# Gate and up projections: the sum W21 + W22 made by the transfers instead of VectorE

## What is computed

```
h2 = rmsnorm(x, norm2_g)                                   # 512 x 1024
x  = x + (silu(h2 @ w_ffn_gate) * (h2 @ w_ffn_up)) @ w_ffn_down   # D_FF = 2816
return rmsnorm(x, final_g)
```

## Time and profile before

| | us |
|---|---|
| median of 3 runs | 698.44 (698.36 to 698.49) |
| the profiled execution | 698.02 |
| its span in the profile | 695.9 |
| busy in the span: PE, DVE, ACT, POOL | 674.3, 484.2, 378.6, 36.6 |
| mean granted clock of PE | 0.994 |

### The profile page before, as it was taken

How to read it: one execution, slowest core, us unless ns; L and a number is a source line. 1 busy time by engine, 2 the same in 40 slices (tenths; PEclk the granted TensorE clock), 3 DMA queues, 4 the chain that set the end, 5 groups by cost and what they waited for, 6 DMA issues and landing times.

```text
span 695.9 us, 10920 instructions
## 1 busy us (share of the span) xinstructions
PE 674.3 (97%) x4042; PEld 602.9 (87%) x4042; DVE 484.2 (70%) x781; ACT 378.6 (54%) x638; POOL 36.6 (5%) x42
## 2 busy tenths in 40 slices
PE   4999999999999999999997999999999999999996
PEld 4998888888888878888897999999999998888884
DVE  4686558787888885845698987878898763333346
ACT  6538577987787872223764545544555552322234
POOL 0000401111121200000000000000000000000000
PEclk9999999999999999999999999999999999999998
DMA  8242221122222226331272334444323313313103
GB/s 292 69 120 79 70 62 27 55 70 66 70 66 85 97 65 268 121 121 61 62 182 70 86 89 122 121 121 121 91 74 80 116 60 122 118 64 121 60 0 122
DMA packets 73694, 67.25 MB, mean 97 GB/s; under 512 B 5887, under 2 KB 64446, under 8 KB 73662
## 3 DMA queue, kind: packets, MB, share of 16 engines
q1 hardware_dynamic: 73646, 66.82, 31.6%
q10 hardware_dynamic: 16, 0.00, 0.0%
HBM read 64.72 MB, written 2.10 MB: 96 GB/s over the span
## 4 chain that ended last, share of the span: by engine, by line
PE 94%; DVE 3%; ACT 2%; DMA 1%; issue 0%; SPq 0%; ACTq 0%; DVEq 0%
PE ps L407 20%; PE ps L409 20%; PE ps L408 20%; PE ps L1704 9%; PE ps L1706 9%; PE ps L1707 9%; PE ps L1613 2%; PE ps L1445 1%; PE ps L1563 1%; PE ps L1560 1%; DMA xt<-in_x_dram 1%; DVE hT_lo L973 1%; DVE w_lo L1240 0%; ACT w_hi L302 0%; DVE f_lo L1251 0%
## 5 line engine op out<-in xcount | busy, mean ns | idle before, releaser
L407 PE MATMUL ps<-hT_hi,w_lo 128*128 128x512 f32 (+1 forms) x288 | 100.2, 348 | 1.1 <-DVE w_lo L312 0.6
L409 PE MATMUL ps<-hT_hi,w_hi 128*128 128x512 f32 (+1 forms) x288 | 98.6, 342 | 0.0
L408 PE MATMUL ps<-hT_lo,w_hi 128*128 128x512 f32 (+1 forms) x288 | 98.5, 342 | 0.0
L1704 PE MATMUL ps<-f_hi,w_lo 128*128 128x256 f32 x320 | 91.4, 286 | 3.9 <-DVE f_lo L1251 3.9
L1706 PE MATMUL ps<-f_lo,w_hi 128*128 128x256 f32 x320 | 91.2, 285 | 0.0
L1707 PE MATMUL ps<-f_hi,w_hi 128*128 128x256 f32 x320 | 91.1, 285 | 0.0
L312 DVE TENSOR_TENSOR w_lo<-raw,w_hi 128x1024 fp32r<-128x1024 f32 (+3 forms) x55 | 64.2, 1173 | 33.0 <-ACT w_hi L302 31.9
L302 ACT ACTIVATE w_hi<-raw 128x1024 fp32r<-128x1024 f32 (+3 forms) x55 | 53.6, 984 | 37.8 <-PE ps L409 36.5
L819 ACT ACTIVATE w_hi<-scr 128x1024 fp32r<-128x1024 f32 x50 | 51.9, 1057 | 37.2 <-PE ps L1707 36.0
L1235 DVE TENSOR_TENSOR w_lo<-raw,w_hi 128x1024 fp32r<-128x1024 f32 x22 | 26.9, 1225 | 63.4 <-ACT w_hi L806 63.4
L407 PE MATMUL ps<-w_hi,f_lo 128*128 128x512 f32 x180 | 70.0, 389 | 0.0
(11 more groups left out here) (195 smaller groups left out, 1501.4 us busy)
## 6 DMA issues: line engine op xcount, KB each, us to landing
raw<-in_w_in_dram SPq DMA_DIRECT2D x12, 1024.0 KB
raw<-in_w_ffn_down_dram SPq DMA_DIRECT2D x11, 1024.0 KB, 4.9
raw<-in_w_ffn_gate_dram SPq DMA_DIRECT2D x10, 512.0 KB, 4.7
raw<-in_w_ffn_up_dram SPq DMA_DIRECT2D x10, 512.0 KB, 5.3
scr<-in_w_ffn_gate_dram SPq DMA_DIRECT2D x10, 512.0 KB, 5.2
scr<-in_w_ffn_up_dram SPq DMA_DIRECT2D x10, 512.0 KB, 6.0
raw<-in_w_out_dram SPq DMA_DIRECT2D x4, 1024.0 KB
xt<-in_x_dram SPq DMA_DIRECT2D x4, 512.0 KB, 6.0
```

The lines of the kernel that those rows point to most:

```text
L407: nc.tensor.matmul(dst, l_lo, r_hi, start=start, stop=False)
L408: nc.tensor.matmul(dst, l_hi, r_lo, start=False, stop=False)
L409: return nc.tensor.matmul(dst, l_hi, r_hi, start=False, stop=stop)
L1704: nc.tensor.matmul(dst, wl[:, k, :], x_hi[:, k, :], start=start and k == 0, stop=False, skip_group_check=True)
```

## The change

S1 is no longer added by DVE. GpSimd issues, for each step and for gate and up each, a transfer of W21 (128 partitions of 4 rows of 512 bytes, 256 KB) to S1's place in `w_sum`, waits until it has landed (`st_base`), and issues a second transfer of W22 that adds to what stands there (`accum_op`), which counts `st_s1`. The first transfer for the next step waits until the low half of c (gate) or d (up) of this step is made, since S1's place is read until then. The sums of the first step are loaded much earlier, when attention no longer needs the place. The raw blocks are loaded as before, so W21 and W22 of every step come twice. The scratch space for GpSimd's transfer descriptors grows from 1024 to 4096 bytes.

On DVE `sums` falls apart: `third` (S3) stays where it was, `second` (S2 = S1 - W11) goes behind the two `corner`, and waits for `st_s1`. ACT's waits count the new order.

```diff
+            def first_sums(j, par, count, first=False):
+                col = slice(j * 256 + P * (2 + STEPS + par), j * 256 + P * (3 + STEPS + par))
+                for m, src in enumerate((w_fg_v, w_fu_v)):
+                    if not first:
+                        pool.wait_ge(w_ready, st_count("cd"[m], j, par - 1))
+                    nc.gpsimd.dma_start(s1_view(m), src[:, 0:4, col]).then_inc(st_base[m], 16)
+                for m, src in enumerate((w_fg_v, w_fu_v)):
+                    pool.wait_ge(st_base[m], count)
+                    nc.gpsimd.dma_start(s1_view(m), src[:, 4:8, col], accum_op=ALU.add).then_inc(st_s1[m], 16)
+
+            pool.wait_ge(vs_ready, HEADS)
+            first_sums(0, 0, 16, first=True)
+            first_sums(0, 1, 32)
+            for j in range(1, STEPS // 2):
+                for par in range(2):
+                    first_sums(j, par, j * 32 + 16 * par + 16)
...
-                nc.vector.tensor_tensor(out(c), w21, w22, ALU.add).then_inc(st_sum, 1)
-                nc.vector.tensor_tensor(out(4 + m), w11, w21, ALU.subtract).then_inc(st_sum, 1)
-                dve.wait_ge(st_sum, j * 16 + 8 * par + 3 * m + 1)
-                nc.vector.tensor_tensor(out(c + 1), out(c), w11, ALU.subtract).then_inc(st_sum, 1)
...
+            def second(m, j, par):
+                dve.wait_ge(st_s1[m], j * 32 + 16 * par + 16)
+                dve.wait_ge(st_in[par][m], j * 32 + 32)
+                nc.vector.tensor_tensor(w_sum[:, 2 * m + 1, :].rearrange("p (k n) -> p k n", k=4), s1_view(m),
+                                        st_raw(par, m)[:, 0:4, 0, :], ALU.subtract).then_inc(st_sum, 1)
...
                 block_lo("g", j, par)
                 corner(0, j, par)
                 if first:
-                    sums(1, nj, npar)
+                    third(1, nj, npar)
+                if not last:
+                    second(0, nj, npar)
                 corner(1, j, par)
+                if not last:
+                    second(1, nj, npar)
...
-    nc = _bacc.Bacc("TRN2", target_bir_lowering=False, num_devices=1, dynamic_dma_scratch_size=1024)
+    nc = _bacc.Bacc("TRN2", target_bir_lowering=False, num_devices=1, dynamic_dma_scratch_size=4096)
```

More of the change, by code:

```diff
@@ L330, in st_raw, with s1_view @@
             return flat.rearrange("p (k i n) -> p k i n", k=KD, i=2)
+        def s1_view(m):
+            return w_sum[:, 2 * m, :].rearrange("p (k n) -> p k n", k=4)
         def st_source(par, tile):
@@ L817, in block_hi @@
                 else:
-                    act.wait_ge(st_sum, j * 16 + 8 * par + {"c": 3, "d": 6, "e": 5, "f": 7, "g": 8}[tile])
+                    act.wait_ge(st_sum, j * 12 + 6 * par + {"e": 2, "c": 3, "d": 4, "f": 5, "g": 6}[tile])
                 nc.scalar.activation(st_split(w_hi, tile), st_source(par, tile), ACT.Copy).then_inc(w_half, 1)
@@ L1252, in t_lo, with third @@
                                         ALU.subtract).then_inc(t_split, 1)
[L1254 to L1260, removed]
-                dve.wait_ge(st_in[par][m], j * 32 + 32)
-                nc.vector.tensor_tensor(out(c), w21, w22, ALU.add).then_inc(st_sum, 1)
-                nc.vector.tensor_tensor(out(4 + m), w11, w21, ALU.subtract).then_inc(st_sum, 1)
-                dve.wait_ge(st_sum, j * 16 + 8 * par + 3 * m + 1)
-                nc.vector.tensor_tensor(out(c + 1), out(c), w11, ALU.subtract).then_inc(st_sum, 1)
+            def third(m, j, par):
+                v = st_raw(par, m)
+                dve.wait_ge(st_in[par][m], j * 32 + 32)
+                nc.vector.tensor_tensor(w_sum[:, 4 + m, :].rearrange("p (k n) -> p k n", k=4), v[:, 0:4, 0, :],
+                                        v[:, 0:4, 1, :], ALU.subtract).then_inc(st_sum, 1)
+            def second(m, j, par):
[3 more added lines that the diff above has]
+                                        st_raw(par, m)[:, 0:4, 0, :], ALU.subtract).then_inc(st_sum, 1)
             def fourth(m, j, par):
                 w12 = st_raw(par, m)[:, 4:8, 0, :]
-                dve.wait_ge(st_sum, j * 16 + 8 * par + 3 * m + 3)
+                dve.wait_ge(st_sum, j * 12 + 6 * par + 3 + m)
                 dve.wait_ge(w_ready, st_count("ab"[m], j, par))
@@ L1297, in step @@
                 feature = j * 2 + par + 2
+                if first:
+                    third(1, 0, 0)
+                    second(0, 0, 0)
+                    second(1, 0, 0)
                 block_lo("c", j, par)
-                if first:
-                    sums(1, 0, 0)
                 block_lo("d", j, par)
@@ L1310, in step @@
                     dve.wait_ge(w_ready, st_count("e", j, par))
-                    sums(0, nj, npar)
+                    third(0, nj, npar)
                 block_lo("f", j, par)
@@ L1361, in _ @@
             block_lo("b", 0, 0)
-            sums(0, 0, 0)
+            third(0, 0, 0)
             first_product(0)
```

1 line of the change is left out of this document (added).

## The result

The changed kernel takes 714.76 us (median of 4 runs, 712.59 to 716.86) against 698.47 for the kernel before beside it: ratio 1.0225, 95% interval 1.0203 to 1.0247. The forecast of no change was wrong. What came is the first rival, "the chain is too long", almost at the price of its example, 715 at L = 14. The profiled execution took 714.0 us, its span 712.1, which is 16.2 more than before.

The account below looks back on a forecast made before the run. PE was taken to bound the ordinary steps, with no hole. DVE's relief, the first step and the transfer chain summed as 0 + 0 + 0 on a median of 698.44: forecast 698.4 us, range 697.2 to 717.

Parts of the forecast that it names:

- the first rival: Ordinary steps: chain too long, DVE stands at `second` of up, PE waits; 715 at L = 14, 761 at most; chance 0.28.
- L: Time from the end of gate's low half of c to the landing of up's S1; taken 9.2 us, bounds 5.7 to 19.1.
- What bounds the kernel: Gate and up stage: PE busy for all 20.17 us of an ordinary step, so less DVE work gives nothing there.
- What leaves DVE: Twenty additions S1 of 0.686 us, 13.7 us busy, leave DVE; PE hides them in ordinary steps: gain 0.
- The first step: PE's one 3.9 us wait: two additions (1.2 us) go where DVE had 3.13 us to spare; gain 0, loss 0.
- The third rival: First step's PE wait shrinks: 697.2 if two additions count, 694.5 if the whole wait goes; chance 0.04.
- The chain's price: GpSimd's two loads and two adding transfers per step: issue 1.3, load 3.2, adding transfer 4.7 us; cost 0.
- the formula: Loss over nine chains in ordinary steps: 9 x (L - 11.8) - 3.1 us, if positive.
- The threshold: DVE's loop in ordinary steps: L + 8.4 over 20.17, so L over 11.8, lengthens each step.
- Second rival: GpSimd can't write descriptors while DVE works, so the chain starts 5.5 us later: L = 14.7, 721; chance 0.04.
- The signs: Changed profile: DVE near 470.5, PE's only stage wait near 3.9; otherwise DVE at second S2, PE at each step's first matmul.
- The danger that I named above all: GpSimd's issue in the chain: 1 us more on each of the four uses up the 2.6 us cover.

Follow-up runs that it names:

- kernel 3: The changed kernel with two places for S1, for even and odd steps, so GpSimd's chain starts one step earlier: 698.64 us, ratio 0.9999.
- Kernel 7: The changed kernel with SP's loads, including the down projection's first two, waiting for the adding transfers: 699.38 us, ratio 0.9997.
- kernel 5: The kernel before, with ACT keeping the four results of c and d earlier in the first step alone: 697.29 us, ratio 0.9978.
- kernel 6: The changed kernel with both kernel 3's two places for S1 and kernel 5's earlier keeping of ACT's results: 694.47 us, ratio 0.9939.
- kernel 2: The changed kernel, but the second transfer overwrites instead of adding, so the sum is left out: 698.98 us, ratio 0.9999.
- kernel 4: The kernel before with DVE's own sums, plus the same forty GpSimd transfers into a place nobody reads: 699.98 us, ratio 1.0012.
- kernel 1: The changed kernel, but SP issues a step's four loads only once that step's adding transfer for up has landed: 700.72 us, ratio 1.0024.

## Why the prediction was wrong, and where it was right

**What bounds the kernel: right.** Ordinary steps have no hole in PE, and less work on DVE gives nothing there. Kernels 3 and 7 show it: DVE has the additions off its list, and the time is that of before.

**What leaves DVE: right.** 471.0 us busy against the 470.5 forecast.

**The first step: right, on its ground too.** The wait is still 3.9 us, and kernel 5 shows that it ends with ACT's kept results. The third rival (the wait shrinks by itself) falls. Sums taken off DVE there are worth 1.2 us only once that wait is gone, as kernel 6 shows.

**The chain's price: this is the step that failed,** and in it one term, the adding transfer "at 4.7". The others came out near: the load at 3.2 landed at 3.4; the issue at 1.3 was 0.78 for a load and 1.30 for an adding transfer. The second adding transfer was to start 4.5 after c's low half and started 5.4 after (481.4 to 486.79), which is 0.9 of the 4.8 us that L was short. The landing, 8.6 for 4.7, is the other 3.9. Put into the formula, this step's L of 14.0 gives a cost of 9 x (14.0 - 11.8) - 3.1 = 16.7 us; the span grew by 16.2. That the two lie so close is in part luck: over the long steps L is 14.0 to 14.8, the point from which a step grows is 12.2 and not 11.8 (see the threshold), and eight chains cost time, not nine. The long steps are 22.37 us on average over seven of them (391.63 to 548.20), which is 2.2 over 20.17 each.

Why was it missed? The prediction names SP's loads beside the adding transfer, but prices them only the other way: how much later SP's loads would land (they do, after 9.1 us instead of 6.0 for up, and nobody waits, as forecast). I took 4.7 by doubling half of a row of 512 KB that had landed in a queue with other loads in it, as if that row held the crowd of this moment. It did not: SP issues two loads at 485.85, 0.5 us after the first adding transfer, and two more at 487.45. Rows for that were at hand: SP's loads start 5.6 us behind the end of the low half of c (477.63 less 472.0) and fill the transfer engines to 1.13 until 486. A chain that starts at 472 and issues its last transfer at 476.5 was bound to meet them. The changed kernel has them nearer still, 4.4 and 6.0 us behind c (485.85 and 487.45 less 481.4) instead of 5.6 and 8.4 (477.63 and 480.43 less 472.0). Only a part of that is the relief of DVE, whose low halves of f and g release SP's loads: in the first ordinary step, before any step is late, and in kernel 3 they come 5.1 and 7.8 or 7.9 us behind c. The rest comes of the lateness itself: DVE, late at c, stands still ahead of f and g no more, where in kernel 2 it still waits 0.30 and 1.06 us for ACT there (477.13 and 480.02). And neither is needed: in kernel 4, with DVE's list and SP's moments as before, the adding transfer for up is as late. Kernel 7 moves them apart and the loss goes; kernel 2 shows that the crowd needs the adding for it.

The Trainium skill, "DMA: Bandwidth & Descriptors", section "Issuing engines are not separate DMA queues", says that transfers of GpSimd and of SP run on the same 16 transfer engines and interleave. The trace agrees: an adding transfer for up lands after 4.7 to 5.1 us in the ordinary steps of kernel 1 and after 8.6 to 9.2 in the changed kernel, beside SP's loads. The Trainium skill's section "Anatomy of one DMA — SWDGE (gpsimd) path" on the same page, from which I had worked out an estimate of 2.6 us for each of the four, is 0.8 short of the loads' 3.4 and far off for the adding ones, so the measurement decides.

**The threshold: right, 0.4 us too low.** L + 8.4 was to exceed the step. The rest of the loop measured 8.0 (21.97 less 14.0), so that the step grows from L = 12.2 on, and kernel 2, with L = 12.0, stands just short of it.

**Second rival, GpSimd locked out by DVE: fell.** The load at 481.75 was issued 0.3 us after its wait ended, in the midst of DVE's row of 480.22 to 483.71, and took 0.78 us there. The Trainium skill's inference in "SBUF — State Buffer", section "Who interferes with whom", that `tensor_tensor` does not lock GpSimd out, agrees with that.

**The signs.** DVE stood at the second S2 and PE at the first matmul of each long step, as named for rival 1. The danger that I named above all, the price of GpSimd's issue, was the wrong term: the issue was no dearer than taken.

**Chances.** With bounds on L from 5.7 to 19.1 and the threshold at 11.8, my 0.64 for no cost rested on one value in between. The first rival had its place and its price right, and the range held the time.

**What stays open.** Beside SP's loads a plain transfer for up takes about 2.9 us more (3.5 to 6.4) and an adding one about 3.7 more (5.0 to 8.7). That the adding one has 528 packets and 2.4 times the engine time goes with that, but which of the two (many packets among SP's, or reading back the place, which no run shows by itself) makes the difference was not tried.

## What to carry to other kernels

Before work is moved from an engine that is not the bound, look for what stands next on the path: 13 us less on DVE were worth nothing until PE waited for DVE, and then the 1.2 us that stood in that place. A chain of transfers that feeds a loop is priced by the moment at which each of them runs: lay its start against the issues of the other queues, and price the crowd in both directions. And where one name stands at a wait with several conditions, as here DVE's low half for ACT's kept result, look at who ended last in the timelines.

## What the hardware showed that was not expected

- An adding transfer of 256 KB (512 pieces of 512 bytes) is 528 packets against 80 of a plain one, takes 33.6 against 14.2 us of transfer-engine time, 1.30 against 0.76 us of GpSimd's time to issue, and lands after 4.5 to 5.1 against 3.2 to 3.8 us with none of SP's loads beside it, and after 8.6 to 9.2 against 6.1 to 7.5 where it runs beside SP's 2 MB of a step.
- In the kernel before, PE's matmuls behind the 3.87 us wait of the first step start 0.21 us apart from 377.94 to 380.86, where 0.12 is usual; behind the shorter waits of kernels 5 and 6 they don't. The stretch behind the wait has a granted clock (the last number but two) of 0.50 in the kernel before and of 1.00 in kernel 5:

```profile
377.70:380.90 3.20, 2.96 (x14) 2.99 (x15) 3.10 (x6) 0.92 (x4) 0.00 (x0) 0.50 0.91 255
```

```profile
381.90:385.10 3.20, 3.20 (x27) 3.20 (x28) 3.20 (x6) 2.53 (x4) 0.00 (x0) 1.00 0.94 264
```

  So after the longer standstill PE was for some 3 us at the lower of its two levels, 1.2 GHz, and not after the shorter one; at 0.12 for 0.21 that stretch holds about 1.2 us. Kernel 5 doesn't pay them, and its wait is 1.0 us shorter; its span is 1.8 us shorter in all, since its slower start (kernel 6) takes some of that back. Each is one execution: in kernel 2's, behind the same wait of 3.9 us, the matmuls stay 0.21 apart until 383.5.
